# Feature-major inputs, outputs and tiled weights for a two-layer encoder trunk on one Trainium2 core

## What is computed

```python
def swiglu(x, wg, wu, wd):
    return (jax.nn.silu(x @ wg) * (x @ wu)) @ wd

for layer in range(2):
    x = x + 0.5 * swiglu(rmsnorm(x, norm_g[layer, 0]), gate[layer, 0], up[layer, 0], down[layer, 0])
    xn = rmsnorm(x, norm_g[layer, 1])
    x = x + (pool_hyena_mixer(xn, ...) if layer == 0 else na_mixer(xn, ..., rpb, w_o))
    x = x + 0.5 * swiglu(rmsnorm(x, norm_g[layer, 2]), gate[layer, 1], up[layer, 1], down[layer, 1])
```

## Time and profile before

| | |
|---|---|
| three runs | 1912.54, 1911.01, 1912.54 us |
| median | 1912.54 us |
| span of the profiled execution | 1909.3 us |
| median less that span | 3.24 us |
| instructions in the span | 23383 |
| granted TensorE clock, mean | 0.998 |
| PE busy | 1887.2 us, 99% |
| DVE busy | 921.8 us, 48% |
| ACT busy | 647.1 us, 34% |
| DMA | 180.34 MB, 94 GB/s |

### The profile page before, as it was taken

How to read it: one execution, slowest core, us unless ns; L and a number is a source line. 1 busy time by engine, 2 the same in 40 slices (tenths; PEclk the granted TensorE clock), 3 DMA queues, 4 the chain that set the end, 5 groups by cost and what they waited for, 6 DMA issues and landing times.

```text
span 1909.3 us, 23383 instructions
## 1 busy us (share of the span) xinstructions
PE 1887.2 (99%) x8579; PEld 1537.3 (81%) x8579; DVE 921.8 (48%) x1166; ACT 647.1 (34%) x859; POOL 79.7 (4%) x63
## 2 busy tenths in 40 slices
PE   6999999999999999999999999999999999999999
PEld 5888888878688888888888888888777788888887
DVE  6444444366555444433544443336776654444321
ACT  4333332233243333322333232225656533333221
POOL 2000000012300000000000000001111000000000
PEclk9999999999999999999999999999999999999999
DMA  6333333243033333333233334323222133333331
GB/s 174 92 98 99 99 105 101 81 133 92 30 91 97 99 97 91 113 97 97 78 99 99 97 91 120 91 83 94 64 82 83 55 100 93 94 99 103 112 107 52
DMA packets 349165, 180.34 MB, mean 94 GB/s; under 512 B 12922, under 2 KB 347525, under 8 KB 349126
## 3 DMA queue, kind: packets, MB, share of 16 engines
q1 hardware_dynamic: 333504, 169.89, 30.6%
q10 hardware_dynamic: 15622, 9.93, 2.0%
HBM read 177.70 MB, written 3.93 MB: 95 GB/s over the span
## 4 chain that ended last, share of the span: by engine, by line
PE 98%; DVE 1%; DMA 0%; ACT 0%; issue 0%; ACTq 0%
PE bank L832 31%; PE bank L836 30%; PE bank L835 30%; PE bank L957 1%; PE bank L1138 1%; PE bank L1122 1%; PE bank L970 1%; PE bank L948 1%; DVE xl L584 0%; DMA vrow<-in_v_params 0%; PE bank L978 0%; PE bank L1110 0%; PE bank L937 0%; PE bank L885 0%; PE bank L1088 0%; PE bank L922 0%
## 5 line engine op out<-in xcount | busy, mean ns | idle before, releaser
L295 DVE TENSOR_TENSOR wl<-raw,wh 128x1024 fp32r<-128x1024 f32 (+1 forms) x296 | 393.4, 1329 | 685.5 <-ACT wh L288 684.1
L832 PE MATMUL bank<-xh,wh 128*128 128x512 f32 x1728 | 682.6, 395 | 6.7 <-DVE xl L584 6.7
L835 PE MATMUL bank<-xl,wh 128*128 128x512 f32 x1728 | 674.0, 390 | 0.0
L836 PE MATMUL bank<-xh,wl 128*128 128x512 f32 x1728 | 673.5, 390 | 0.0
L288 ACT ACTIVATE wh<-raw 128x1024 fp32r<-128x1024 f32 (+1 forms) x296 | 333.7, 1127 | 515.4 <-PE bank L836 515.0
L832 PEld LDWEIGHTS bank<-xh,wh 128*128 128x128 f32 x1728 | 324.8, 188 | 85.9 <-issue 12.9
L836 PEld LDWEIGHTS bank<-xh,wl 128*128 128x128 f32 x1728 | 325.0, 188 | 68.6
L835 PEld LDWEIGHTS bank<-xl,wh 128*128 128x128 f32 x1728 | 325.1, 188 | 66.4 <-issue 1.4
L832 PE MATMUL bank<-hh,wh 128*128 128x512 f32 x704 | 274.9, 391 | 0.0
L836 PE MATMUL bank<-hh,wl 128*128 128x512 f32 x704 | 274.0, 389 | 0.0
L835 PE MATMUL bank<-hl,wh 128*128 128x512 f32 x704 | 273.9, 389 | 0.0
(11 more groups left out here) (144 smaller groups left out, 1023.4 us busy)
## 6 DMA issues: line engine op xcount, KB each, us to landing
raw<-in_ffn_w_gate SPq DMA_DIRECT2D x88, 512.0 KB, 3.8
raw<-in_ffn_w_up SPq DMA_DIRECT2D x88, 512.0 KB, 3.9
raw<-in_ffn_w_down SPq DMA_DIRECT2D x64, 704.0 KB, 4.5
raw<-in_w_qkv SPq DMA_DIRECT2D x24, 512.0 KB, 3.8
raw<-in_w_in_ab SPq DMA_DIRECT2D x16, 512.0 KB, 3.9
raw<-in_w_out_ab SPq DMA_DIRECT2D x8, 512.0 KB, 3.6
raw<-in_w_o SPq DMA_DIRECT2D x8, 512.0 KB, 3.6
braw<-bias_by_column ACTq DMA_DIRECT2D x16, 192.0 KB, 3.8
```

The source lines that it names most:

```text
L295: dve.tensor_tensor(wl[w][:, 0:ph.kt, :], raw[r][:, 0:ph.kt, :], wh[w][:, 0:ph.kt, :].bitcast(F32), ALU.subtract).then_inc(low, 1)
L832: pe.matmul(out, wh[w][:, k, :], hi[:, at, :], start=start, stop=False)
L835: pe.matmul(out, wh[w][:, k, :], lo[:, at, :], start=False, stop=False)
L836: return pe.matmul(out, wl[w][:, k, :], hi[:, at, :], start=False, stop=stop)
```

## The change

The host lays out `x` as [128, 8 x 512], feature-major, in the order of the tile `x`, so it is loaded into its place. The parameters come as [128, 106], straight into `vec`. The weights come as tiles, so that a unit's load has one contiguous row per partition (4 KB; 5.5 KB in down phases) where it had 8 or 11 rows of 512 bytes. The outputs are written from `x` in 1 KB rows, feature-major. The transposes of `vrow`, `xrow` and the outputs are gone, with their copies. GpSimd's part in norm 0 goes to DVE. The first iteration of up0 is written out by hand: all eight first loads are issued at once, ACT makes all of xh before any square, and the mean of norm 0 moves from unit (0, 1) to unit (0, 2), its root and everything behind it likewise.

```diff
@@ sync
-                sp.dma_start(xrow[:, n % 2 * 2:n % 2 * 2 + 2, half],
-                             (a["x_sample"] if n % 2 else a["x_prompt"])[0].rearrange("(t p) c -> p t c", p=P)[:, :, half])\
-                  .then_inc(x_in[n], 16)
+            def bring_x(n):
+                sp.dma_start(x[:, 2 * n:2 * n + 2, :].rearrange("p k t -> p (k t)"),
+                             a["x_tokens"][:, 2 * n * TOK:2 * (n + 1) * TOK]).then_inc(x_in[n], 16)
+            def bring_weights(ph, i, j):
+                sp.dma_start(raw[j][:, 0:ph.kt, :].rearrange("p k c -> p (k c)"),
+                             unit_source(ph, i, j).rearrange("o p c -> (o p) c")).then_inc(raw_in[j], 16)
+            bring_x(0)
+            bring_weights(phases[0], 0, 0)
+            for n in range(1, 4):
+                bring_x(n)
+            for j in range(1, 4):
+                bring_weights(phases[0], 0, j)
@@ scalar, down3
-                        act.wait_ge(y_mm, d + 1)
-                        act.wait_ge(y_out[s], 32 * i + STORE_CREDIT)
-                        act.activation(ua[s][:, :], bank[2 + s][:, :], ACT.Copy).then_inc(y_copied, 1)
-                        act.wait_ge(y_copied, d + 1 + COPY_CREDIT)
+                        act.wait_ge(evac, ph.group(i, j) + 1 + EVAC_CREDIT)
                         for n, y in enumerate((y_prompt, y_sample)):
+                            act.dma_start(y[:, bass.ds(d, 1), :], x[:, bass.ds(d, 1), n * SEQ:(n + 1) * SEQ])\
+                               .then_inc(y_out, 16)
@@ scalar, start
+            act.wait_ge(vec_in, 16)
             for d in range(KD):
-                act.wait_ge(evac, d + 1 + EVAC_CREDIT)
+                act.wait_ge(x_in[d // 2], 16)
+                act.activation(xh[:, d, :], x[:, d, :], ACT.Copy, scale=col(V_NORM + d)).then_inc(xh_done, 1)
+                if d == 1:
+                    split_high(act, phases[0], 0, 0)
+            split_high(act, phases[0], 0, 1)
+            for d in range(KD):
+                if d == 4:
+                    split_high(act, phases[0], 0, 2)
                 if d >= 2:
                     act.wait_ge(acc_done, d - 1)
-                residual_parts(0, d, d % 2)
-                if d == 1:
-                    split_high(act, phases[0], 0, 0)
-                if d == 4:
-                    split_high(act, phases[0], 0, 1)
+                act.activation(sqtmp[:, d % 2, :], x[:, d, :], ACT.Square).then_inc(sq_done, 1)
+            split_high(act, phases[0], 0, 3)
+            act.wait_ge(const_in, 16)
+            norm_std(0)
+            split_high(act, phases[0], 1, 0)
+            evacuate(phases[0], 0, 0)
+            evacuate(phases[0], 0, 1)
+            split_high(act, phases[0], 1, 1)
+            evacuate(phases[0], 0, 2)
+            evacuate(phases[0], 0, 3)
 
             for r in range(DR):
...
@@ vector, start
             for d in range(KD):
-                dve.wait_ge(x_mm, d + 1)
-                dve.tensor_copy(x[:, d, :], bank[d][:, :]).then_inc(evac, 1)
-            split_low(dve, phases[0], 0, 0)
+                part_low(0, d)
+                if d == 1:
+                    split_low(dve, phases[0], 0, 0)
+            split_low(dve, phases[0], 0, 1)
             for d in range(KD):
-                part_low(0, d)
                 if d == 4:
-                    split_low(dve, phases[0], 0, 1)
+                    split_low(dve, phases[0], 0, 2)
+                add_squares(0, d, d % 2)
+            split_low(dve, phases[0], 0, 3)
+            norm_factor(0)
+            evacuate(phases[0], 0, 0)
+            split_low(dve, phases[0], 1, 0)
+            evacuate(phases[0], 0, 1)
+            sums_cleared(0)
+            evacuate(phases[0], 0, 2)
+            split_low(dve, phases[0], 1, 1)
+            evacuate(phases[0], 0, 3)
@@ tensor
-            pe.transpose(bank[7][:, 0:V_ALL], vrow[:, :], cst[0:V_ALL, C_ID:C_ID + V_ALL]).then_inc(vec_mm, 1)
...
-                for t in range(TT):
-                    last = pe.transpose(bank[d][:, t * P:(t + 1) * P], xrow[:, t, d * P:(d + 1) * P], ident)
-                last.then_inc(x_mm, 1)
...
-                    if name == "down3" and j == 2:
-                        return {8: lambda: turn_y(2 * i, 0)}
-                    if name == "down3" and j == 0 and not (isinstance(i, int) and i == 0):
-                        return {8: lambda: turn_y(2 * i - 1, 1)}
...
+                    if name == "up0":
+                        unit(ph, 0, 0, waits=[(xl_done, k + 1) for k in range(KD)])
+                        unit(ph, 0, 1)
+                        unit(ph, 0, 2, hooks={6: lambda: norm_mean(0)})
+                        rest = range(3, ph.per)
```

More of the change, by code:

```diff
@@ L87, in plan @@
               Phase("w_o", 2, 4, KD, [0, 1, 2, 3]), up(3), down(3)]
-    unit, group, uses = 0, KD, [0] * 4
+    unit, group, uses = 0, 0, [0] * 4
     for n, ph in enumerate(phases):
@@ L254, in load @@
                     sp.wait_ge(low, ph.unit(i, j) - 2 + LOW_CREDIT)
-                    sp.dma_start(raw[j][:, 0:ph.kt, :], unit_source(ph, i, j)).then_inc(raw_in[j], 16)
+                    bring_weights(ph, i, j)
             for ph in phases:
-                if ph.name == "w_in":
+                if ph.name == "up0":
+                    with sp.Fori(1, ph.iters) as i:
+                        load(ph, i)
+                elif ph.name == "w_in":
                     for i in range(ph.iters):
@@ L538, in _ @@
                         act.activation(ah[:, 4 + c, :], x0[:, c, :], ACT.Copy).then_inc(ah_done, 1)
-            for s in range(2):
-                act.wait_ge(y_out[s], 16 * KD + STORE_CREDIT)
+            act.wait_ge(y_out, 32 * KD)
         @block.vector
@@ L589, in residual_low, with add_squares @@
                 part_low(norm, d)
+                add_squares(norm, d, parity)
+            def add_squares(norm, d, parity):
                 dve.wait_ge(sq_done, chunk_base(norm) + d + 1)
-                dve.wait_ge(acc_done, chunk_base(norm) + d)
+                if not isinstance(d, int) or norm or d:
+                    dve.wait_ge(acc_done, chunk_base(norm) + d)
                 dve.tensor_tensor(sqacc[:, :], sqacc[:, :], sqtmp[:, parity, :], ALU.add).then_inc(acc_done, 1)
@@ L653, in evacuate @@
                     dve.wait_ge(unit_done, ph.unit(i, j) + 1 + UNIT_CREDIT)
-                    out = ga[parity][:, :] if ph.name == "down3" else x[:, bass.ds(d, 1), :]
+                    out = x[:, bass.ds(d, 1), :]
                     dve.scalar_tensor_tensor(out=out, in0=bank[b][:, :], scalar=factor, in1=x[:, bass.ds(d, 1), :],
@@ L916, in turn_u @@
                 last.then_inc(ut_mm, 1)
-            def turn_y(d, s):
-                pe.wait_ge(evac, by["down3"].group0 + d + 1 + EVAC_CREDIT)
-                pe.wait_ge(y_copied, d - 1 + COPY_CREDIT)
-                for t in range(TT):
-                    last = pe.transpose(bank[2 + s][:, t * P:(t + 1) * P], ga[s][:, t * P:(t + 1) * P], ident)
-                last.then_inc(y_mm, 1)
             def attention(p, projects, attends, last_one):
@@ L1099, in _ @@
                     body(i, False)
-                if name == "down3":
-                    turn_y(KD - 1, 1)
                 if name == "w_in":
@@ L1145, in _ @@
         def _(pool):
-            pool.wait_ge(low, LOW_CREDIT)
-            for d in range(KD):
-                pool.wait_ge(sq_done, d + 1)
-                if d:
-                    pool.wait_ge(acc_done, d)
-                pool.tensor_tensor(sqacc[:, :], sqacc[:, :], sqtmp[:, d % 2, :], ALU.add).then_inc(acc_done, 1)
             ph = by["w_in"]
```

85 lines of the change are left out of this document (38 added, 47 removed).

## The result

The changed kernel took 1919.2 us (1918.1 to 1920.4) beside 1911.8 us for the kernel before in the same session: 0.4% slower, ratio 1.004, 95% interval 1.0025 to 1.0054. Forecast were 1904.5 us, a range of 1896 to 1908.7, and faster. The span went from 1909.3 to 1916.3 us; the profiled execution of the changed kernel took 1918.07 us, the shortest of its four runs.

What follows compares the result with a forecast made beforehand. PE, busy 99%, was taken to bound the kernel. 12.4 - 0.7 - 6.2 - 2.1 + 3.3 + 1.3 = 8.0 us off the 1909.3 us span gives 1901.3, plus 3.2 to the median: 1904.5 us, range 1896 to 1908.7.

Steps and rivals of the forecast that it cites:

- What bounds the kernel: Whole program: PE is busy 99%, so only time taken from PE's own sequence or its idle ends counts.
- The start, gain 12.4: Up to unit (0, 1): it starts at 18.0 us instead of 30.4, PE's first work at half rate; gain 12.4 us.
- The norm, loss 0.7: Before unit (1, 0): mean one unit later and root's table load exposed make PE wait; loss 0.7 us.
- The bias transfers, loss 6.2: End of iteration 0: their issues hold ACT 7.9 us, delaying unit (1, 2)'s weight split; PE loses 6.2 us.
- The clock, loss 2.1: After the bias stall: PE's clock falls to half rate for 3 to 5.6 us; loss 2.1 us (0 to 2.8).
- The outputs, gains 3.3 and 1.3: down3 and the end: seven output turns gone gain 3.3 us; final transposes and ACT's copy gone gain 1.3 us.
- The step that failed: Middle of the program: DMA, DVE and ACT are off the path, so longer rows gain nothing there; priced zero.
- The fourth rival: All 296 units: long weight rows' SBUF writes hold up PE's reads; 0.08 us more per unit gives 1920 us; chance 0.06.
- The check named for it: Steady phase: if two units' interval is not 10.88 us, the rival of stretched units is right.

Runs made afterwards that it cites:

- e11: The changed kernel with gqk as a column of seed, so the tiles behind lie exactly 512 bytes lower than before the change: 1904.4 us, ratio 0.9957.
- e7: The changed kernel with only the seven bias transfers moved from ACT's program to SP's, behind the eight first loads: 1910.7 us, ratio 0.9996.
- e1: The changed kernel with seed 16 columns wide in place of 8, so every tile behind it lies 32 bytes higher: 1908.7 us, ratio 0.9987.
- e5: The changed kernel with seed 32 columns wide, so tiles behind it start at a multiple of 128 bytes: 1919.0 us, ratio 1.0038.
- e10: The changed kernel with seed 64 columns wide, so the moved tiles lie 256 bytes lower than before the change: 1903.3 us, one run.
- e2: The kernel before with an unused 32-byte tile behind gqk, old weight rows kept: 1928.4 us, ratio 1.0091.
- e6: The kernel before with an unused 64-byte tile behind gqk, weight rows kept at 512 bytes: 1918.1 us, one run.
- e9: The kernel before with an unused 32-byte tile ahead of everything, so all tiles lie 32 bytes higher and keep their distances: 1911.8 us, one run.
- e12: The changed kernel with bias transfers on SP, both table loads ahead of their waits and gqk as a column of seed: 1893.4 us, ratio 0.9902.

## Why the prediction was wrong

- **What bounds the kernel**: right. PE stayed at 99%, and every microsecond found or lost in the traces was PE's.
- **The start, gain 12.4**: right in each step. Unit (0, 1) began at 18.04 for 18.0 (in the timeline 17.88, a gain of 12.5). The half rate lasted from 10.19 to about 14.8, as chosen between the two bounds. The profile's clock row reads 1.00 for that stretch, while the matmuls are 0.43 us apart and 0.23 from 14.8 on, so the choice against the row was right. Its length is a matter of the execution: in e11 the matmuls are 0.43 us apart until 16.5, and unit (0, 1) begins at 18.75. The parameters landed 4.7 us after the issue, against 7.66 for the 106 rows.
- **The norm, loss 0.7**: 0.4 in e7, as in the changed kernel.
- **The bias transfers, loss 6.2**: 5.29 in the trace. The DVE chain ahead of them was 0.4 us shorter than counted (hh at 42.35, S+18.9 with S at 23.5) and the issues took 7.23. **The clock, loss 2.1**: the records show 0.50 from 52.3 to 55.7, which costs half of that, 1.7. This too varies by execution: in e1, e5, e10 and e11, which have the same start, the clock read 0.50 for 6.8 us, and 3.8 to 6.1 us of that lay behind the stall, a loss of 1.9 to 3.0. The stall itself was 5.5 to 5.8 us there. e7, 8.5 us faster without both, fits the upper end.
- **The outputs, gains 3.3 and 1.3**: right. From the first split of down3 to the end of the span e11 and e10 gain 4.7 and 4.8 us for the 4.6. In e11 2.9 us of it come between the first and the last split, and the last DVE addition is followed by the output issue with 0.03 us between.
- **The step that failed** is the sentence that DMA, DVE and ACT in the middle are not on the path, "so 4 KB rows in place of 512 bytes gain nothing there. What is left is the start ..., the output turns, and the last 2 us", and with it the price of zero for the middle of the program. It took PE's own 0.68 us for a block as a constant. The change moved the operands of 79 units (64 down, 8 w_out, 7 w_o; the eighth of w_o takes its weights from the third buffer, which moved along) relative to their weights, and each of their 2472 matmuls took 6.7 ns more: 14.1 us in down phases and 2.4 in w_out and w_o by that count, 16.5 together. Measured, from the first split of down0 to the end of the span, the changed kernel takes 1658.2 us and e10, the same program at full speed, 1641.8, so 16.4 us. (qkv has 8 units on the third buffer as well, whose operands stayed; what they lost is within a few tenths.) The trace of before has no row on it, but the change has: a tile of 512 bytes goes and one of 32 comes in the middle of the allocation.
- **The fourth rival** had the place (every unit stretches) and the sign that would show it, but not the cause. It was written for long rows, which e2 and e6 refute, and was given 0.06. Its price was also miscounted: 0.08 us on each of 296 units is 23.7 us, so 1928 us and not 1920. The check named for it, two steady units at 10.88, would have missed it in up phases, where nothing had moved; the interval in down phases showed it.

With the placement put back, the changed kernel takes 1904.4 us in e11 and 1903.3 in e10, beside the 1904.5 of the forecast. That it meets e11 so closely is luck. The sum took 8.0 us off the span; e10's profile has 7.8 off and e11's 6.2, since its clock fell in w_o. To the span the forecast then added 3.2 us, the median less the profiled span. But each run on record lies 1.8 us over its own span (1904.88 and 1903.1 in e11's profiled one), so 1.5 of the 3.2 only meant that the profiled execution of the kernel before was faster than its median run. What the sum counted was therefore right within 2 us, and one term of about 16 us was not in it.

What stays open is why the distance counts. The records of PE and PEld overlap (99% and 80% of the span), so PE reads a moving operand while it loads the next weights, and a clash of the two reads is a candidate; no run here separates it from others. The distance is not the whole of it either: at 64 bytes the three products of a block differ. In two chunks of down1 in e1 the next matmul starts 231.7 ns after hh x wh, 229.0 after hh x wl and 226.0, full speed, after hl x wh, though hh and hl are equally far from wh modulo 256. Offsets other than 0, 32, 64, 128 and 224 were not tried, nor a distance between hh and hl.

## What to carry to other kernels

When a change adds, drops or resizes an on-chip tile, list where every tile behind it has moved, against the tiles it is multiplied with, before costing anything else; here 3% of a third of the matmuls cost more than the stall and the clock behind it. Compare the start-to-start distance of matmuls in each phase of the two traces, not the busy share, which hides it. And a DMA issue is work of the engine that issues it: put long series of them on a queue whose next duty is far away, and look at what stands behind them in that engine's program.

## What the runs showed of the hardware

- The start-to-start distance of back-to-back float32r matmuls of 128x512 was 226.7 or 233.3 ns by where moving and stationary tile lie relative to each other: full speed at an offset of 0 modulo 256 bytes against the kernel before, 3% slower at 32, 128 and 224, 1% slower at 64 (the last is a mean: in e6 the group hh x wh had a mean duration of 395 ns, hh x wl 392, hl x wh 388).
- The absolute address did not count in the one shift that was tried: e9, with every tile 32 bytes higher, ran like the kernel before, 1911.8 us.
- The clock row read 1.00 from 10.2 to 14.8 us in the changed kernel, while its first matmuls started 0.43 us apart; behind the 5.3 us stall it read 0.50 for 3.4 us, in e1, e5, e10 and e11 for 6.8.
- Seven DMA issues of 1024 rows of 256 bytes held the issuing engine 7.2 us on ACT at 42 us, where the DMA engines had been 13% busy in the 4 us before, and 13.7 us on SP at 5 us, amid 4 MB of loads.
- A table load in front of an activation with two waits took over one of them and went from hidden to exposed, 1.28 us each time. With both loads ahead of their waits, e12's PE waits for DVE were 1.1 and 0.4 us shorter.
- The eight first loads ran at 365 to 418 GB/s from 5 to 14 us, in 4 KB rows. The old start, with rows of 512 bytes to 2 KB, had 398 GB/s at 5 to 6 us and 288 to 293 at 11 to 13 us.
